# Dilated attention's projections: a fourth 256x256 square in seven products instead of eight, with the work of the vector engine in another order

## What is computed

```python
def dilated_attention(h, w_qkv, q_gain, k_gain, w_o, rel_bias):
    qkv = (h @ w_qkv).reshape(B, S, N_SW_GROUPS, SW_GROUP_COLS)      # three groups, 8 heads of q, k (128) and v (256)
    ...
    for g, (window, dil) in enumerate(SW_GROUPS):
        q, k, v = jnp.split(qkv[:, :, g], [nqk, 2 * nqk], axis=-1)
        q = rmsnorm(q.reshape(B, S, N_HEADS, HEAD_DIM), q_gain[g])
        k = rmsnorm(k.reshape(B, S, N_HEADS, HEAD_DIM), k_gain[g])
        ...
        p = jnp.exp(logits - m)
        l = jnp.sum(p, axis=-1, keepdims=True)
        o = jnp.einsum('bnrhqk,bnkrhe->bnqrhe', (p / l).astype(v.dtype), vv)
    ...
    o = alpha[0][..., None] * outs[0] + alpha[1][..., None] * outs[1] + alpha[2][..., None] * outs[2]
    return o.astype(h.dtype).reshape(B, S, ATTN_WIDTH) @ w_o
```

## Time and profile before

| | us |
|---|---|
| median of 3 runs | 2487.33 (2486.79 to 2487.71) |
| the profiled execution | 2487.73 |
| its span | 2485.9 |
| TensorE busy in the span | 2477.3 |
| VectorE busy | 2162.0 |
| ScalarE busy | 1472.0 |
| one head of the dilated attention (heads 1 to 6) | 71.58 |
| the same, VectorE busy | 56.9 |

### The profile page before, as it was taken

How to read it: one execution, slowest core, us unless ns; L and a number is a source line. 1 busy time by engine, 2 the same in 40 slices (tenths; PEclk the granted TensorE clock), 3 DMA queues, 4 the chain that set the end, 5 groups by cost and what they waited for, 6 DMA issues and landing times.

```text
span 2485.9 us, 29114 instructions
## 1 busy us (share of the span) xinstructions
PE 2477.3 (100%) x11403; PEld 2061.0 (83%) x11403; DVE 2162.0 (87%) x2389; ACT 1472.0 (59%) x1436; POOL 44.3 (2%) x54
## 2 busy tenths in 40 slices
...
GB/s 284 195 187 170 169 186 147 228 202 248 191 251 205 208 187 215 178 238 201 158 156 170 195 198 187 189 169 155 139 249 203 232 217 204 233 185 199 244 172 159
DMA packets 359401, 491.24 MB, mean 198 GB/s; under 512 B 20005, under 2 KB 200437, under 8 KB 356832
## 3 DMA queue, kind: packets, MB, share of 16 engines
...
...
## 4 chain that ended last, share of the span: by engine, by line
PE 93%; DVE 4%; ACT 1%; DMA 1%; issue 1%; ACTq 0%; SPq 0%
PE psum L2073 47%; PE psum L2077 24%; PE psum L1923 5%; PE psum L1914 5%; PE psum L1915 5%; PE psum L2176 2%; PE psum L2303 1%; DVE w_lo L1143 1%; PE psum L1872 0%; DVE w_lo L1151 0%; PE psum L2267 0%; PE psum L2301 0%; PE psum L2275 0%; ACT w_hi L684 0%; DMA w_raw<-in_f_w_up 0%
## 5 line engine op out<-in xcount | busy, mean ns | idle before, releaser
L2073 PE MATMUL psum<-w_hi,xT 128*128 128x512 f32 x4456 | 1115.0, 391 | 0.0
L2073 PEld LDWEIGHTS psum<-w_hi,xT 128*128 128x128 f32 x4456 | 833.3, 188 | 171.5 <-issue 0.2
L671 ACT ACTIVATE w_hi<-w_raw 128x2048 fp32r<-128x2048 f32 (+1 forms) x350 | 631.3, 1810 | 390.6 <-PE psum L2077 258.3
L1143 DVE TENSOR_TENSOR w_lo<-w_raw,w_hi 128x2048 fp32r<-128x2048 f32 (+1 forms) x332 | 704.9, 2145 | 55.3 <-ACT w_hi L671 54.7
L2077 PE MATMUL psum<-w_lo,xT 128*128 128x512 f32 x2228 | 583.9, 389 | 1.1 <-DVE w_lo L1151 0.9
L2077 PEld LDWEIGHTS psum<-w_lo,xT 128*128 128x128 f32 x2228 | 417.8, 188 | 89.6 <-DVE w_lo L1151 2.2
L1151 DVE TENSOR_TENSOR w_lo<-w_raw,w_hi 128x2048 fp32r<-128x2048 f32 (+1 forms) x174 | 375.8, 2176 | 49.8 <-ACT w_hi L684 49.4
L684 ACT ACTIVATE w_hi<-w_raw 128x2048 fp32r<-128x2048 f32 (+1 forms) x174 | 315.7, 1827 | 154.2 <-PE psum L2077 68.1
L2073 PE MATMUL psum<-w_hi,mixT 128*128 128x512 f32 x992 | 265.3, 389 | 0.0
L1914 PE MATMUL psum<-w_hi,xT 128*128 128x512 f32 x624 | 245.1, 393 | 1.0 <-DVE phase L1296 1.0
L1915 PE MATMUL psum<-w_hi,xT 128*128 128x512 f32 x624 | 243.1, 390 | 0.0
...
## 6 DMA issues: line engine op xcount, KB each, us to landing
...
w_raw<-in_b_w_qkv SPq DMA_DIRECT2D x256, 128.0 KB, 2.7
...
```

The lines of the kernel that those rows point to most:

```text
L671: nc.scalar.activation(w_hi[:, slot, cols], w_raw[:, slot, cols], ACT.Copy).then_inc(hi_ready, 1)
L1143: nc.vector.tensor_tensor(w_lo[:, slot, cols], w_raw[:, slot, cols], w_hi[:, slot, cols], ALU.subtract).then_inc(lo_ready, 1)
L2073: pe.matmul(o, x[:, h, P * m:P * (m + 1)], hi, start=start and h == 0, stop=False)
```

## The change

`THREE` stays for the MLPs. The heads get a list of their own, `FOUR`: std 0, std 1, std 2, one 4, one 5, sum 4, sum 5, one 6, one 7, sum 6, sum 7, std 3. A head has 16 entries then, and four squares in seven products. The x of a fourth pair is mixed for this layer alone (`X_MIXED`). So that `mixT` can hold four pairs, the constants move into `small`, the shared buffer `phase` shrinks from 14848 to 14336 columns, and buffers in it move; the MLPs' mixed h has two buffers where it had three; a few waits come in for memory that is now shared. On DVE, from head 1 on, `b_norm` stands ahead of the split of chunk 3, the reciprocal of the softmax moves to entry 4 behind a sum of weights, and `b_combine` and `b_sum` stand ahead of the splits of their entries.

```diff
+FOUR = (("std", 0), ("std", 1), ("std", 2), ("one", 4), ("one", 5), ("sum", 4), ("sum", 5), ("one", 6), ("one", 7), ("sum", 6),
+        ("sum", 7), ("std", 3))
-MIXED = (4, 5, 6)
+MIXED = (4, 5, 6, 7)
+X_MIXED = (3, 3, 4, 3)
...
-B_ENTRIES = tuple(("all", j) for j in range(4)) + THREE
-MIX_PAIRS = len(MIXED)
+B_ENTRIES = tuple(("all", j) for j in range(4)) + FOUR
+MIX_PAIRS, H_MIX = len(MIXED), 2
...
+B_ADD_AT = (4, 6, 7)
+PHASE = 14336
...
-        b_lg = part(6144, 1152)
+        b_lg = part(0, 1152)
...
-                    if k // 2 in MIXED:
+                    if k // 2 in MIXED[:X_MIXED[n]]:
...
             def b_take_p1(c, h, odd):
                 chunk_used(act, c)
+                at_least(act, b_tp, h)
...
-                if f >= MIX_PAIRS:
-                    dve.wait_ge(h_mix_lo, mixes_made(layer, f - MIX_PAIRS))
+                if f >= H_MIX:
+                    dve.wait_ge(h_mix_lo, mixes_made(layer, f - H_MIX))
...
                 if j == steps[1]:
                     dve.wait_ge(b_scores, h + 1)
+                    dve.wait_ge(b_vheld, h + 1)
...
                     nc.vector.tensor_scalar(nmx[:, 0:2], mx[:, 0:2], -1.0, None, ALU.mult).then_inc(b_nmx, 1)
+                if j == steps[1] + 1:
                     dve.wait_ge(b_exp, h + 1)
                     nc.vector.reciprocal(rden[:, 0:2], den[:, 0:2]).then_inc(b_rden, 1)
...
                         b_add_weights(c + B_ONES[0], c + B_SUMS[0])
+                    if h > 0 and e in (0, B_STEPS[1] + 1):
+                        b_attend(e, h - 1, B_STEPS, 4 * odd)
+                    if e == B_HEAD - 2:
+                        b_combine(c + B_SUMS[-1], h, odd)
+                    if e == B_HEAD - 1:
+                        b_sum(c + e, h, odd)
                     split_ahead(c, e, BO0)
-                    for one, to in zip(B_ONES[1:], B_SUMS[1:]):
-                        if e + LEAD + 3 == one:
+                    for at, one, to in zip(B_ADD_AT, B_ONES[1:], B_SUMS[1:]):
+                        if e == at:
                             b_add_weights(c + one, c + to)
...
-                    else:
+                    elif e not in (0, B_STEPS[1] + 1):
                         b_attend(e, h - 1, B_STEPS, 4 * odd)
...
-                    if e == B_HEAD - 2:
-                        b_combine(c + B_SUMS[-1], h, odd)
-                    if e == B_HEAD - 1:
-                        b_sum(c + e, h, odd)
```

More of the change, by code:

```diff
@@ L283, in trunk @@
         ident = sb("ident", [P, P])
-        gains = sb("gains", [P, GAINS])
         conv = sb("conv", [P, 2, 4, 2 * FB])
-        sub_g = sb("sub_g", [P, 2])
-        nlam = sb("nlam", [P, 1])
-        small = sb("small", [P, 160])
+        small = sb("small", [P, 144])
+        gains, sub_g, nlam = small[:, 64:64 + GAINS], small[:, 138:140], small[:, 140:141]
         psum = ctx.enter_context(nc.psum_tensor("psum", [P, 8, 512], F32))
-        phase = sb("phase", [P, 14848])
+        phase = sb("phase", [P, PHASE])
         def part(at, *dims):
             n = int(np.prod(dims))
-            assert at + n <= 14848
+            assert at + n <= PHASE
             v = phase[:, at:at + n]
@@ L312, in trunk @@
         a_a = part(6144, 768)
-        a_aT = part(6912, 6, P)
-        a_o = part(7680, 4, VD)
-        a_bias = part(8704, H, SEQ)
-        a_oT = part(10752, KB, SEQ)
+        a_aT = part(2048, 6, P)
+        a_o = part(6912, 4, VD)
+        a_bias = part(8192, H, SEQ)
+        a_oT = part(10240, KB, SEQ)
         b_raw = part(0, G * M, 512)
@@ L321, in trunk @@
         b_v = part(4608, G * M, VD)
-        b_lg = part(6144, 1152)
-        b_pT = part(7296, 9, P)
-        b_sq = part(7296, G * M, 256)
-        b_bias = part(8960, G, SEQ)
-        b_mask = part(9728, G, SEQ)
-        b_row = part(10496, SEQ)
-        b_oT = part(10752, KB, SEQ)
+        b_lg = part(0, 1152)
+        b_pT = part(6144, 9, P)
+        b_sq = part(6144, G * M, 256)
+        b_bias = part(7680, G, SEQ)
+        b_mask = part(8448, G, SEQ)
+        b_row = part(9216, SEQ)
+        b_oT = part(10240, KB, SEQ)
         hT = part(0, FB, SEQ)
         u = part(11264, 2 * M, 512)
-        x_f32 = part(11264, 2 * MIX_PAIRS, SEQ)
-        mix_f32 = part(12800, 4, MIX_PAIRS, P)
+        x_f32 = part(10240, 2 * MIX_PAIRS, SEQ)
+        mix_f32 = part(12288, 4, MIX_PAIRS, P)
         c_gate = part(13312, 4, SEQ)
-        h_mix = part(13312, MIX_PAIRS, 4, P)
+        h_mix = part(13312, H_MIX, 4, P)
         t_lam = part(5120, 4, HD)
@@ L350, in trunk @@
         n_ss, n_r, n_t = small[:, 16:28], small[:, 28:40], small[:, 40:52]
-        mx, nmx = small[:, 52:56], small[:, 56:60]
-        den, rden, rneg = small[:, 60:64], small[:, 64:68], small[:, 68:70]
-        q_ss, q_r, q_t = small[:, 96:112], small[:, 112:128], small[:, 128:144]
-        o_ss, o_r, o_t = small[:, 144:148], small[:, 148:152], small[:, 152:156]
+        mx, nmx, den, rden = (small[:, at:at + 2] for at in (52, 54, 56, 58))
+        q_ss, q_r, q_t = small[:, 16:32], small[:, 32:48], small[:, 48:64]
+        o_ss, o_r, o_t = small[:, 16:20], small[:, 20:24], small[:, 24:28]
         a_mx, a_nmx, a_den, a_rden, a_rneg = (small[:, at:at + n] for at, n in (
             (16, 8), (24, 8), (32, 8), (40, 8), (48, 4)))
-        lam_s, lam_e = small[:, 76:78], small[:, 78:80]
+        lam_s, lam_e = small[:, 16:18], small[:, 18:20]
         x_in = [sem(f"x_in{q}") for q in range(4)]
@@ L744, in a_squares @@
                 at_least(act, a_scores, p)
+                at_least(act, a_pv, p)
                 for i in range(2 * M):
@@ L968, in h_mix_high @@
                 act.wait_ge(h_mixed, mixes_made(layer, f))
-                nc.scalar.activation(mixT[:, :, f % MIX_PAIRS, 0, :], h_mix[:, f % MIX_PAIRS, :, :], ACT.Copy).then_inc(h_mix_hi, 1)
+                nc.scalar.activation(mixT[:, :, f % MIX_PAIRS, 0, :], h_mix[:, f % H_MIX, :, :], ACT.Copy).then_inc(h_mix_hi, 1)
             def down_take_p1(layer, p):
@@ L1100, in _ @@
             act.wait_ge(warm_ready, 1)
-            nc.scalar.activation(small[:, 80:81], t_warm[:, 0:1], ACT.Copy)
+            nc.scalar.activation(small[:, 14:15], t_warm[:, 0:1], ACT.Copy)
             split_piece(0, 0)
@@ L1472, in b_out_proj @@
                 for j in range(OUT):
+                    if j == B_LAST_STEPS[1] + 1:
+                        b_attend(j, H - 1, B_LAST_STEPS)
                     split(c + j + LEAD)
@@ L1475, in b_out_proj @@
                         split_o(b_oT, j + 2)
-                    b_attend(j, H - 1, B_LAST_STEPS)
+                    if j != B_LAST_STEPS[1] + 1:
+                        b_attend(j, H - 1, B_LAST_STEPS)
                     if j == B_LAST_STEPS[-1]:
```

20 lines of the change are left out of this document (10 added, 10 removed).

## The result

| | before | after |
|---|---|---|
| median, us | 2487.52 (2486.79 to 2487.92, 4 runs) | 2506.85 (2504.17 to 2511.48, 4 runs) |
| profiled execution; span | 2487.73; 2485.9 | 2511.48; 2509.7 |
| mean granted clock of the runs | 1.0 | 0.996, 0.998, 0.999, 0.997 |

The ratio is 1.008 [1.0062, 1.0098]: 19.3 us slower, where no change was forecast and the range ended at 2493.0. The page of after: span and engines, then the chain that ended last, and the group of the first products of an "all" chunk.

A forecast was written before the change was run, and what follows sets the result against it. TensorE was taken as the bound, busy 2477.3 of 2485.9 us. Matmuls removed -5.44, heads' ends +0.6, head 0 +1.1, output projection +3.5 gave -0.2 us: forecast 2487.1, range 2482.4 to 2493.0.

The forecast's parts named there:

- (1): TensorE in the heads: 24 matmuls fewer at 0.227 us each, -5.44 us.
- (2a): Middle of the head: DVE's copies of the probabilities still in time with 0.3 us left, no cost.
- (2b): The eight fast entries: DVE's splits over 2 us ahead of TensorE each, no cost.
- (2d): DVE's norm and copy of k in the head: done 0.3 us before TensorE wants it, no cost.
- (2c): Loads behind std 3: no cover left before `b_combine`, 0.1 us at each of six heads' ends, +0.6 (0 to 3.0).
- Head 0's end: End of head 0: costs nothing, as no attention holds its splits and std 3 is loaded 3 us sooner.
- (3): Head 0's fifth entry: TensorE waits for DVE's copy in `b_take`, +1.1 us (0.9 to 1.3).
- (4): Output projection: TensorE waits for `b_combine` at the start and the norm before the transposes, +3.5 us (2.0 to 4.5).
- C: Heads' ends fall behind later loads: 1.3 us at each of six, output projection 4.6, in all +8.1, 2495.4; chance 0.2.
- B: Nothing waits at heads' ends or output projection: -5.44 us, 2481.9 to 2483.0; chance 0.12.
- D: Middle of the head loses its 0.3 us cover: 0.3 a head, seven heads, +2, 2489.2; chance 0.08.
- A: Loads come closer together, 2.5 us instead of 3.28, no head's end waits: -1.8, 2485.5; chance 0.12.

The follow-up runs named there:

- the last version: Changed kernel with `b_take_p1`, `b_combine`, `b_sum` an entry earlier, `mix_low` behind `b_take`'s copy, squares (heads, output projection) and output projection's norm ahead of splits: 2482.48 us, 0.9981.
- experiment 4: Changed kernel with the old list of squares in the heads (three in seven products), keeping new memory layout and DVE order: 2490.39 us, 1.0011.
- experiment 9: Changed kernel with ACT's `b_take_p1` and DVE's `b_combine` one entry earlier, ahead of the split of the next head's chunk 0: first run 2492.02 us, 1.0018.
- Experiments 1: Changed kernel with the load of each head's last std cut to two of its six DMAs: 2489.25 us, 1.0006.
- experiment 7: Changed kernel, but SP issues each head's chunk 1 only when its chunk 0 has landed: 2540.92 us, one execution.

## Why the prediction was wrong

- **(1) What goes: right.** 24 matmuls fewer; where nothing waits, a head takes 70.9 us, and the last version gains 5.1 of the 5.44.
- **(2a), (2b), (2d): right for this kernel,** no wait in the middle of a head or for `w_lo` amid the fast entries beyond 0.16 us once. The covers of 0.3 were as thin as I had them: experiment 4 has lost that of (2a), experiment 9 that of (2d).
- **(2c) The loads: this step failed, by its size.** Std 3 is issued at 1304.94, 57.35 us behind head 2's first matmul, 1.7 of them its slow stretch: 55.6, where I had 1371.9 - 1316.6 = 55.3. It lands 6.2 later, as I had it; chunk 1 comes one pitch behind chunk 0, 3.25 us, as I had it. But chunk 0 was ready 8.4 us behind its first issue (1316.28 - 1307.91; 7.4 to 8.4 over the heads), where I put 6.3; even the 7.0 that I took for the upper end of the range was passed at every end. In the prediction's clock `b_combine` stands at 1389.4 instead of 1386.8 (1316.59 + 1322.13 - 1247.59 - 1.7), and 2.1 of these 2.6 us are that landing. The wait is 2.45 there and 1.96 on the mean, not 0.1. Experiments 1 and 7 give the cause as far as it is known: 0.7 us by the std's DMAs ahead, 0.8 by chunk 1's behind.
- **The rows that would have told it were in the trace of before.** The landing of the earlier trace rows isn't that of a load alone, though the expectation of experiment 7 calls it so. It is chunk 0 at the end of head 2, with std 7 issued 4.8 us ahead of it and chunk 1 2.5 behind; in after these distances are 3.0 and 1.6. SP there (std 7, chunk 0, chunk 1), and then SP and ACT at the end of head 3:

```profile
1295.16 2.93 SPq L532 DMA_DIRECT2D w_raw<-in_b_w_qkv  x6
...
1299.95 1.47 SPq L528 DMA_DIRECT2D w_raw<-in_b_w_qkv  x3
...
1302.48 1.47 SPq L528 DMA_DIRECT2D w_raw<-in_b_w_qkv  x3
...
1366.74 3.97 SPq L532 DMA_DIRECT2D w_raw<-in_b_w_qkv  x6
1371.53 7.74 SPq L528 DMA_DIRECT2D w_raw<-in_b_w_qkv  x9
...
1378.61 1.92 ACT L684 ACTIVATE w_hi<-w_raw 128x2048 fp32r<-128x2048 f32 x1 [0.88 <-DMA w_raw<-in_b_w_qkv]
```

Chunk 0 took 7.1 us at the end of head 3, issued as far behind the std's first DMA but with chunk 1 only 1.8 behind it (1373.28); so 6.3 was the shorter of two landings at this place. Chunk 1 (1381.87) came 15.1 behind the std's first DMA, or 13.3 if chunk 0 is issued 1.8 sooner. From 1371.9 that is 1385.2 to 1387.0, not 1384.4: a wait of 0.8 to 2.6 us at each end. I had used this head's rows for the pitch and not for the landing.
- **Head 0's end** costs 1.2 us, not nothing: std 3 isn't loaded 3 us sooner there but is issued 15.7 ahead of the head's end (1172.86 - 1157.20), against 15.5 at head 2's, and 3.0 ahead of chunk 0 as everywhere.
- **The clock was no term of the sum.** It was full throughout before, so no row showed what a wait of 2 us does to it. It cost 9.7 us of the profiled execution's 23.8, and 2.5 to 10 of each run. Without it these four runs would be at 2499 to 2502, still outside the range.
- **(3) Head 0: right,** 1.02 us against 1.1.
- **(4) The output projection: right in size by luck, wrong in place.** 3.9 and 5.3 us, all at its start, where I had 3.5 to 4.9 split over start and transposes. `b_combine` began at 1693.08, 1.1 us behind TensorE's 1692.01, where I had it 0.5 to 1.9 ahead. Its norm ended at 1709.35; at full clock TensorE would have been there at 1706.7 and waited 2.7 more, 6.5 in all. The slow stretch filled that time and cost 3.0 itself.
- **Rivals.** C is what happened, by its mark (heads 1 to 6 take 73.5 to 75.3 us, over 71.6) and by the path through `b_take_p1`; but the std in front did not land later, only the loads behind it. I gave it 0.2, and priced an end at 1.3 instead of 2.0, with no clock. B fell, since TensorE waited at every head's end, and D has no wait in the middle of a head. A fell in the heads: the pitch stayed at 3.25 us with the loads close together, 1.05 MB / 3.25 = 323 GB/s. The output projection's chunks of one DMA did come every 2.5 us (split at 1687.99 and 1690.48), and moved, in GB/s (last number):

```profile
1685.00:1690.00 5.00, 5.00 (x23) 4.14 (x23) 2.35 (x2) 2.07 (x2) 0.00 (x0) 1.00 1.02 400
```

Of the two ceilings of the Trainium skill ("DMA: Bandwidth & Descriptors", Where 436 GB/s comes from), 358 is passed here, so the measurement decides against it as a limit of this kernel; 435 isn't reached over these 5 us. What holds the heads' loads of three DMAs at 323 stays open.
